# Four small buffers of a two-layer decoder kernel move to other SBUF addresses

## The reference

```
for l in range(2):
    h = rmsnorm(x, mix_norm_g[l])
    a_b, a_c, a_x, s_u, s_v, q, k, v, gates = split_cols(h @ w_in[l])     # 1024 x 7168
    ya = a_b * conv3(a_c * a_x)                        # causal short convolution, 512 channels
    yb = gelu(s_u) * (tril(sgu_w) @ layernorm(gelu(s_v)) + sgu_b)   # chunks of 128 tokens
    yc = stick_breaking(rmsnorm(q), rmsnorm(k), v)     # 8 heads of 64, causal
    merged = sum_i sigmoid(gates_i + b_gate_i) * (y_i @ w_branch_out[l, i])
    x = x + merged @ w_o[l]
    g, u = split(rmsnorm(x, ffn_norm_g[l]) @ w_gate_up[l])          # 1024 x 2*2816
    x = x + (silu(g) * u) @ w_down[l]
```

## Time and profile before

| | |
|---|---|
| median of 3 runs | 1708.37 us (1707.94 to 1708.78) |
| the profiled execution's own time | 1708.78 us |
| its span, first to last instruction | 1707.0 us |
| mean granted TensorE clock | 0.994 of full |
| TensorE matmul busy | 1679.0 us, 98% |
| TensorE weight load busy | 1396.0 us, 82% |
| VectorE (DVE) busy | 979.7 us, 57% |
| ScalarE (ACT) busy | 751.2 us, 44% |
| GpSimd (POOL) busy | 250.9 us, 15% |
| moved by DMA | 163.84 MB, mean 96 GB/s |

### The profile page before, as it was taken

One profiled execution on the slowest core, in us unless ns is written; L12 is line 12 of the kernel. 1 busy time (PEld: TensorE's weight loads), 2 busy tenths in 40 slices (PEclk: granted clock), 3 DMA queues, 4 the chain that ended last, 5 costly groups with the idle time before them and its releaser, 6 DMA issues.

```text
span 1707.0 us, 22660 instructions
## 1 busy us (share of the span) xinstructions
PE 1679.0 (98%) x7651; PEld 1396.0 (82%) x7651; DVE 979.7 (57%) x1181; ACT 751.2 (44%) x1050; POOL 250.9 (15%) x225
## 2 busy tenths in 40 slices
PE   6999999999999999999999999999999999999997
PEld 5788888888888888888877888888888888888886
DVE  4687786554555434434658877765546544443447
ACT  5476766433333223313346776763333432232223
POOL 5233231000030000000333233200002100000004
PEclk9999999999999999999999999999999999999999
DMA  5322222323333333333333222223333333333334
GB/s 155 93 75 86 87 73 87 92 87 97 105 98 96 94 95 98 98 99 98 111 115 98 75 86 86 86 69 99 92 98 99 99 98 96 92 95 99 98 99 135
DMA packets 310544, 163.84 MB, mean 96 GB/s; under 512 B 5472, under 2 KB 306648, under 8 KB 310488
## 3 DMA queue, kind: packets, MB, share of 16 engines
q1 hardware_dynamic: 308184, 158.94, 31.7%
q10 hardware_dynamic: 2304, 4.20, 0.7%
HBM read 156.83 MB, written 2.10 MB: 93 GB/s over the span
## 4 chain that ended last, share of the span: by engine, by line
PE 91%; DVEq 2%; DVE 2%; ACT 2%; POOLq 1%; issue 1%; ACTq 0%; POOL 0%; DMA 0%; SPq 0%
PE bank L513 27%; PE bank L514 27%; PE bank L517 27%; PE z L584 2%; DVEq L1499 2%; PE z L517 1%; PE z L513 1%; PE z L514 1%; DVE w_lo L1120 1%; PE z L557 1%; ACT xg_hi L802 1%; POOLq L424 1%; PE z L558 1%; POOLq L419 1%; PE misc L600 1%
## 5 line engine op out<-in xcount | busy, mean ns | idle before, releaser
L513 PE MATMUL bank<-xg_hi,w_hi 128*128 128x512 f32 x1600 | 631.3, 395 | 3.5 <-DVE xg_lo L1502 1.8
L514 PE MATMUL bank<-xg_lo,w_hi 128*128 128x512 f32 x1600 | 625.1, 391 | 0.0
L784 ACT ACTIVATE w_hi<-raw 128x1024 fp32r<-128x1024 f32 (+1 forms) x299 | 309.3, 1036 | 539.6 <-DMA raw<-in_w_gate_up 219.3
L1120 DVE TENSOR_TENSOR w_lo<-raw,w_hi 128x1024 fp32r<-128x1024 f32 (+1 forms) x299 | 402.5, 1348 | 39.6 <-ACT w_hi L784 22.8
L517 PE MATMUL bank<-xg_hi,w_lo 128*128 128x512 f32 x1600 | 396.1, 389 | 1.4 <-DVE w_lo L1120 1.4
L513 PEld LDWEIGHTS bank<-xg_hi,w_hi 128*128 128x128 f32 x1600 | 301.8, 189 | 67.3 <-DVE xg_lo L1502 2.2
L514 PEld LDWEIGHTS bank<-xg_lo,w_hi 128*128 128x128 f32 x1600 | 301.7, 189 | 62.5 <-issue 1.2
L517 PEld LDWEIGHTS bank<-xg_hi,w_lo 128*128 128x128 f32 x1600 | 300.4, 188 | 64.0 <-DVE w_lo L1120 1.9
L1125 DVE TENSOR_TENSOR S<-bank,rstd 128x512 f32<-128x512 f32 x152 | 104.9, 690 | 263.2 <-PE bank L517 262.8
L513 PE MATMUL bank<-mid_hi,w_hi 128*128 128x512 f32 x480 | 187.1, 390 | 0.0
L514 PE MATMUL bank<-mid_lo,w_hi 128*128 128x512 f32 x480 | 186.9, 389 | 0.0
(11 more groups left out here) (191 smaller groups left out, 1667.2 us busy)
## 6 DMA issues: line engine op xcount, KB each, us to landing
raw<-in_w_in SPq DMA_DIRECT2D x112, 512.0 KB, 3.7
raw<-in_w_gate_up SPq DMA_DIRECT2D x88, 512.0 KB, 3.8
raw<-in_w_down SPq DMA_DIRECT2D x48, 512.0 KB, 3.6
raw<-in_w_o SPq DMA_DIRECT2D x19, 512.0 KB, 3.5
raw<-in_w_branch_out SPq DMA_DIRECT2D x16, 512.0 KB, 3.5
raw<-in_w_branch_out SPq DMA_DIRECT2D x16, 256.0 KB, 2.6
gates<-in_x SPq DMA_DIRECT2D x4, 512.0 KB, 5.6
mix_hi<-yb_hi ACTq DMA_DIRECT2D x8, 256.0 KB, 2.3
```

Of the source, the lines that this page charges most:

```text
L513: mm(dst[:, :], wh[:, k0 + k, :], his[k], start=(k % per == 0), stop=False)
L514: mm(dst[:, :], wh[:, k0 + k, :], los[k], start=False, stop=False)
L784: af(w_hi[at.slot(c)][:, 0:kc, :], raw[at.slot(c)][:, 0:kc, :], ACT.Copy).then_inc(hi_done, 1)
L1120: tt(w[:, 0:kc, :], r[:, 0:kc, :], h[:, 0:kc, :].bitcast(F32), ALU.subtract).then_inc(lo_done, 1)
```

## The change

Four declarations move up in the list of `sb` calls; their shapes stay. `eps`, `par` and `gain0` are now allocated before `ya_hi`, and `conv_in` before `N0`. `N2`, `sq_sum` and `sq_one` are names for parts of tiles and move with their line. No instruction, wait, loop or transfer is edited.

```
         sw_lo = sb("sw_lo", [P, KC, P], F32R)
+        eps = sb("eps", [P, 1])
+        par = sb("par", [P, 64])
+        gain0 = sb("gain0", [P, KD])
         ya_hi = sb("ya_hi", [P, KC, T], F32R)
...
         KT = sb("KT", [P, T])
+        conv_in = sb("conv_in", [P, 2 + T])
         N0 = sb("N0", [P, T])
         N1 = sb("N1", [P, T])
+        N2 = conv_in[:, 2:2 + T]
+        sq_sum, sq_one = S2[:, :], N1[:, :]
 
         over = plan[0]
...
         plan[0] = max(plan[0], over + 16 * 4 * T)
-        conv_in = sb("conv_in", [P, 2 + T])
-        N2 = conv_in[:, 2:2 + T]
-        sq_sum, sq_one = S2[:, :], N1[:, :]
-        eps = sb("eps", [P, 1])
-        par = sb("par", [P, 64])
-        gain0 = sb("gain0", [P, KD])
         assert plan[0] <= nc.sbuf_usable_end, plan[0]
```

## The result

The changed kernel takes 1719.38 us (median of four runs, 1716.7 to 1720.0) against 1708.57 us before (1707.94 to 1709.39): 10.8 us more. The ratio is 1.006, with a 95% interval of 1.0046 to 1.0076. It is slower, by three times the 0.2% that tell a change from none, and outside the forecast range.

The account below looks back on a forecast made before the run. The prediction took TensorE's matmul count times their distance, plus a start and an end, to bound the kernel. All terms of the change were 0, so 1707.0 + 1.8 less 0.4 gave 1708.4 us, range 1706.3 to 1710.6.

Parts of the forecast that it names:

- What bounds the kernel: Whole kernel: TensorE busy 1679.0 of 1707.0 us, so time is number of matmuls times their distance, plus a start and an end.
- the TensorE term: Matmuls on moved operands, 1440 on `mid` and 576 on the branches: claimed to cost the same at new addresses, 0 us.
- The slower rival: Matmuls on `mid`: operand start off a 64-byte multiple costs 13.4 ns each, 19.3 us more, 1727.7; nearly all of 0.07.
- ScalarE and VectorE: Their reads and writes of moved tiles: starts off a 64-byte multiple claimed free, and the work covered anyway, 0 us.
- POOL: Adds ahead of TensorE's 4.1 us wait: claimed unchanged by the new distance between their operands, 0, bounds 1.6 us either way.
- the faster rival: POOL's adds get cheaper, the 4.1 us wait vanishes and the clock stays up: 6.6 us less, 1701.8; within 0.06.
- Transfers: First load of x and last store, through moved `gates`: between 0 and 0.1 us at each end, taken as 0.
- The sum: Whole kernel: span 1707.0 plus 1.8 around it plus 0 gives 1708.8 profiled; median 0.4 lower, 1708.4 us.

## Why the prediction was wrong, point by point

**What bounds the kernel** held: the time is the number of matmuls times their distance. That is why 3% on a fifth of them (1440 of 7651) is 9.5 us.

**The step that failed** is the TensorE term: "I put this term at 0". It was taken from "So a move by a multiple of 512 is free", but the change moves `mid` by 2400 bytes and the branches by 320, and neither is a multiple of 512. The premise held (at 2560 bytes, five times 512, `mid` is back at 327.4 us); it said nothing of 2400, as the prediction itself noted ("What no row shows"), and no price for it entered the range. The rows were read rightly and asked too little. All groups of the earlier trace rows have one time at different places, but in all of them operand and weights leave the same remainder by 256, so they were one case seen five times and could not speak about any other. The same 0 stood for the branches (320 bytes), with only their multiple of 64 behind it; their term is 1.5 us. The term of `mid` is 9.5 us.

**The slower rival** was the right place (TensorE, `mid`), and its sign in the profile came out as written: eight of L517 at 1.86 us on `mid`, 1.81 us on `xg`. Its price of 13.4 ns per matmul was double the 6.7 ns measured, and its condition was wrong: not a start off a multiple of 64, which the changed kernel with `mid` 32 bytes further and the kernel before with all tiles 32 further both refute, but the distance to `w_hi` by 256. What it had right is that nothing covers TensorE; its price was a guess that no row bore out. Against it I had held the odd starts on ScalarE and VectorE; those rows were no evidence on TensorE, for ScalarE and VectorE kept 632 and 693 ns on the very `mid` tiles whose matmuls got longer.

**ScalarE and VectorE**: term 0, right. On the moved `conv_in`, after:

```profile
L797 ACT ACTIVATE conv_in<-N x20: 630/633/635, 35.4 to 1355.9; 128x512 f32<-128x512 f32 x20
...
L1324 DVE SCALAR_TENSOR_TENSOR S<-conv_in,par,S x8: 750/752/754, 136.6 to 1134.1; 128x512 f32<-128x512 f32 x8
```

**POOL**: term 0, right. The least time of an add is 1261 ns after against 1267, and the wait at L614 is 4.2 us against 4.1:

```profile
L421 POOL TENSOR_TENSOR S<-S,N x35: 1261/1761/2092, 10.1 to 1710.9; 128x512 f32<-128x512 f32 x35
```

So the faster rival is out: a new distance between the two operands of an add changed next to nothing. The rule of the Trainium skill (SBUF — State Buffer, Who interferes with whom) on the port pair of VectorE and GpSimd gives 0 for this term, and the trace agrees (1261 against 1267 ns). The same section says that TensorE has two independent read ports, for the moving operand and for the weights, and never waits on anyone. As far as addresses go, the measurement differs: with the weights alone moved by 32 bytes against `xg`, the start of one matmul on `xg` to the next took 233 ns instead of 227. Whether the ports are where that time goes isn't shown.

**Transfers**: term 0, right within 0.1 us. The last store is waited for 1.9 us as before:

```profile
SPq L111 <- DMA out_x<-gates: 1.9, 1, 1.9
```

The estimate of 0.06 us from the Trainium skill (DMA: Bandwidth & Descriptors, How a descriptor splits into AXI transactions) is below what this row can tell.

**The sum with the measured terms**: 9.5 (`mid`) + 1.5 (branches) = 11.0 us, against 10.8 us between the medians. That they agree this closely is partly chance: two waits got shorter by 1.4 us together (L772, L1502), and the `xg` row still grew by 1.7.

**What stays open.** That the distance between the operand and the weights decides is shown, by moving either alone and both together. Why is only argued: a weight load of 188 ns runs beside each matmul, its own time doesn't change, and the matmuls wait a little when the two read at unlike remainders. Whether the load of the next weights or their layout (one block each 512 bytes) makes the period of 256 wasn't tried, nor steps finer than 32 bytes. The runs with `mid` alone at 32, 128 and 192 are 5.9 to 6.8 us slower at the whole, though 9.4 to 9.9 us are added in their `mid` stages. For the profiled execution at 32, which is 4.0 us longer than that of before, the traces account for the gap. Shorter waits at L772 and L1502 are 1.6 us of it. The rest is the clock behind three waits of TensorE (4.1 us at L614, 2.0 us twice at L557), in these stretches (columns as in the earlier trace rows, the clock is the third value from the end). Before:

```profile
31.00:37.00 6.00, 5.93 (x13) 4.08 (x14) 0.84 (x2) 3.51 (x5) 1.04 (x5) 0.55 0.02 3
80.00:92.00 12.00, 10.04 (x42) 8.31 (x41) 11.13 (x14) 7.24 (x11) 3.70 (x2) 0.86 0.16 45
916.00:930.00 14.00, 12.04 (x51) 9.96 (x50) 12.90 (x16) 9.15 (x14) 3.90 (x2) 0.88 0.13 39
```

With `mid` at 32:

```profile
31.00:37.00 6.00, 6.00 (x19) 4.18 (x19) 0.99 (x2) 3.67 (x5) 1.03 (x4) 0.76 0.01 4
80.00:92.00 12.00, 10.02 (x49) 8.16 (x48) 11.47 (x14) 7.16 (x11) 2.47 (x2) 1.00 0.21 57
916.00:930.00 14.00, 12.03 (x58) 9.83 (x57) 13.06 (x16) 9.11 (x14) 3.90 (x2) 1.00 0.20 59
```

Counted by the starts of the same matmuls, the run at 32 gains about 1.3, 1.5 and 0.9 us there, 3.7 in all, and 9.5 - 1.6 - 3.7 = 4.2. This is not an effect of the address: with `mid` at 256 the three clocks are 0.72, 1.00 and 0.88, and with the change 0.52, 0.86 and 0.91, nearly those of before, so the comparison of before and after stands clear of it. How often each kernel's other executions had the higher clock is not known, so for the medians the gap is explained only in kind.

## What to carry to other kernels

An allocator's order can be a tuning decision. Where TensorE is the bound and loads new weights for each matmul, as here (only 128x512 float32 matmuls with weights of 128x128 were measured), give the moving operand and the weights the same remainder by 256 bytes (round the sizes of all small tiles up to 256, or put them behind the large ones), and look at the distance of matmuls by tile after any edit that moves addresses. Here no placement beat the kernel before: distance 0 is the best of seven, and the kernel before has it for all its large products. When many rows agree, ask what they have in common before taking them as proof that a quantity doesn't matter.

## What the runs showed of the hardware that was not expected

- The distance from one matmul of 512 float32 columns to the next depends on the addresses of its moving operand and of the weights, by their difference past a multiple of 256 bytes: 226.7 ns at 0, 229 ns at 64, 233 ns at 32, 96, 128, 192 and 224. The clock granted was 1.00 of full in a stretch of `mid` units (455 to 511 us) at 0, at 32, at 96 and at 128.
- Moving both by the same 32 bytes costs nothing (ratio 0.9998).
- 32 bytes between weights and operands cost 2.2% of a whole kernel when all its large products are concerned (1745.72 us).
- Behind a wait of TensorE of 2 us (L557) the granted clock over 80 to 92 us was 0.86 in some executions and 1.00 in others, worth 1.5 us. Both values stand at distance 0 (0.86 before, 1.00 with `mid` at 256).
